# Modulation of layer 0's gate and of layer 1 moved from TensorE to row products summed on VectorE, and GpSimd's low parts of the first z pieces put ahead of the first inverse

## The reference, cut to what matters

```python
def ada_mod(cond, w, b):
    m = jax.nn.silu(cond) @ w + b
    return jnp.split(m[..., None, :], 3, axis=-1)

for i in range(DEPTH):
    shift, scale, gate = ada_mod(c, ada_w[i], ada_b[i])
    c_shift, c_scale, c_gate = ada_mod(c_ctx, ada_w[i], ada_b[i])
    h = rms_norm(x, norm_w[i]) * (1.0 + scale) + shift
    hc = rms_norm(ctx, norm_w[i]) * (1.0 + c_scale) + c_shift
    ...                       # i = 0: ab_mixer, i = 1: dn_mixer
    x = x + gate * o
    if need_ctx_out:
        ctx = ctx + c_gate * oc
```

## Time and profile before

| | |
|---|---|
| median of 3 runs | 2652.07 us (2651.2 to 2652.84) |
| the profiled execution | 2654.93 us, its span 2653.1 us |
| mean granted clock of TensorE | 0.96 of full speed |
| PE busy | 2447.0 us, 92% |
| DVE busy | 1028.2 us, 39% |
| ACT busy | 1132.7 us, 43% |
| POOL busy | 1179.7 us, 44% |
| chain that ended last | PE 71%, POOL 12%, DVE 6% |
| DMA | 352.15 MB, mean 133 GB/s |

### The profile page before, as it was taken

How to read it: one execution, slowest core, us unless ns; L and a number is a source line. 1 busy time by engine, 2 the same in 40 slices (tenths; PEclk the granted TensorE clock), 3 DMA queues, 4 the chain that set the end, 5 groups by cost and what they waited for, 6 DMA issues and landing times.

```text
span 2653.1 us, 59556 instructions
## 1 busy us (share of the span) xinstructions
PE 2447.0 (92%) x26092; PEld 2019.1 (76%) x26092; DVE 1028.2 (39%) x2211; ACT 1132.7 (43%) x2034; POOL 1179.7 (44%) x653
## 2 busy tenths in 40 slices
PE   6899999999999968999999999999999999986997
PEld 1477777777778847788878887888788878875997
DVE  1222222232230066444444444444444444443222
ACT  3423333333342245465346445643564356433443
POOL 2232333332335554643664365436544654451444
PEclk9899999999999969999999999999999999998999
DMA  9645444554443123223222322232223222314653
GB/s 397 259 168 195 170 182 183 207 199 189 167 183 95 56 87 106 89 66 105 96 97 66 105 96 95 68 105 91 97 71 105 89 96 74 105 49 172 226 182 121
DMA packets 98915, 352.15 MB, mean 133 GB/s; under 512 B 10720, under 2 KB 15200, under 8 KB 96224
## 3 DMA queue, kind: packets, MB, share of 16 engines
q1 hardware_dynamic: 98656, 348.34, 37.2%
HBM read 336.11 MB, written 12.19 MB: 131 GB/s over the span
## 4 chain that ended last, share of the span: by engine, by line
PE 71%; POOL 12%; DVE 6%; issue 4%; ACT 4%; DMA 3%; SPq 0%; POOLq 0%; DVEq 0%; ACTq 0%
PE bank L550 8%; PE bank L552 8%; PE bank L551 8%; PE bank L819 5%; PE bank L713 4%; PE bank L715 4%; PE bank L714 4%; POOL wl L401 4%; PE bank L526 3%; POOL scratch L2127 3%; PE bank L753 3%; POOL scratch L2147 3%; PE bank L754 3%; PE bank L755 3%; PE bank L1125 2%
## 5 line engine op out<-in xcount | busy, mean ns | idle before, releaser
L401 POOL TENSOR_TENSOR wl<-raw,wh 128x1024 fp32r<-128x1024 f32 x214 | 512.1, 2400 | 777.1 <-ACT wh L396 777.1
L713 PE MATMUL bank<-hh,wh 128*128 128x512 f32 (+1 forms) x1040 | 410.4, 395 | 22.4 <-POOL hl L2117 17.7
L396 ACT ACTIVATE wh<-raw 128x1024 fp32r<-128x1024 f32 x233 | 246.2, 1059 | 377.0 <-PE bank L755 229.9
L342 POOL TENSOR_TENSOR wl<-raw,wh 128x1024 fp32r<-128x1024 f32 x85 | 208.0, 2459 | 421.3 <-ACT wh L337 421.3
L550 PE MATMUL bank<-hh,wh 128*128 128x512 f32 x960 | 386.7, 403 | 5.9 <-POOL wl L342 3.6
L715 PE MATMUL bank<-hh,wl 128*128 128x512 f32 (+1 forms) x1040 | 385.5, 371 | 0.0
L714 PE MATMUL bank<-hl,wh 128*128 128x512 f32 (+1 forms) x1040 | 384.4, 370 | 0.0
L552 PE MATMUL bank<-hh,wl 128*128 128x512 f32 x960 | 376.8, 392 | 0.0
L551 PE MATMUL bank<-hl,wh 128*128 128x512 f32 x960 | 376.3, 392 | 0.0
L713 PEld LDWEIGHTS bank<-hh,wh 128*128 128x128 f32 x1040 | 199.7, 192 | 61.5 <-POOL hl L2117 15.2
L753 PE MATMUL bank<-wh,hh 128*128 128x256 f32 x512 | 166.3, 325 | 79.8 <-POOL wl L401 79.8
(11 more groups left out here) (273 smaller groups left out, 4487.1 us busy)
## 6 DMA issues: line engine op xcount, KB each, us to landing
raw<-w_in SPq DMA_DIRECT2D x259, 512.0 KB, 3.6
raw<-w_ada SPq DMA_DIRECT2D x123, 512.0 KB, 6.0
raw<-w_out SPq DMA_DIRECT2D x84, 512.0 KB, 3.7
scratch<-w_ada SPq DMA_DIRECT2D x69, 512.0 KB, 6.0
scratch<-keep_g SPq DMA_DIRECT2D x16, 1024.0 KB, 6.1
scratch<-w_in SPq DMA_DIRECT2D x23, 512.0 KB, 6.9
scratch<-xT SPq DMA_DIRECT2D x2, 4096.0 KB, 12.6
keep_y<-scratch SPq DMA_DIRECT2D x30, 256.0 KB, 2.4
```

What stands on the lines that cost most here:

```text
L342: eng.tensor_tensor(fl[h % SPLIT], ring[ring_slot("half", h)], fh[h % SPLIT].bitcast(F32), ALU.subtract)\
L396: eng.activation(buffers(s)[0], raw[:, s % RAW, :], ACT.Copy).then_inc(sem("rear_hi"), 1)
L401: eng.tensor_tensor(buffers(s)[1], raw[:, s % RAW, :], buffers(s)[0].bitcast(F32), ALU.subtract)\
L713: pe.matmul(ps, w[:, k * P:(k + 1) * P], hhv[:, kk, t0:t1], start=first and k == k0, stop=False)
```

## The change

Three things.

**The later modulation goes to VectorE.** The weights of the 64 tiles (gate of layer 0, tiles 32 to 47, shift, scale and gate of layer 1, tiles 48 to 95) are stored transposed, output columns on the partitions, contraction along the row: `w_late`, in 128 units of 128x1024, first half of the contraction (b = 0) for all tiles, then second half. The condition comes as two rows spread over all partitions (`crow`, half of the contraction at a time), ScalarE puts SiLU on it. VectorE multiplies a unit with a row and sums along it (`tensor_tensor_reduce`), two pieces of 512, for both conditions, or for the latent one alone in layer 1's gate; the sums run on in `mod`. All `ada`, `ada_rows`, `ada_sum` and `ada_add` of the mixing loop go. `GAPS` says how many units stand at which of four places of a group on VectorE: ahead of the q norm, behind it, behind the normed v, at the end. 83 units stand in the mixing loop, three each behind the merges of the output tiles.

**The ring is split.** Halves use 4 slots, units the other 2; SyncE's one queue still carries both, and the load of a unit waits until the unit two before it is done.

**GpSimd in layer 1** makes the low part of z piece 0 before the last two couplings and that of piece 1 before the first inverse.

The diff, cut to its core:

```diff
+LATE = list(range(2 * KT, 6 * KT))
+UNITS = [(tile, b) for b in range(2) for tile in LATE]
+NLATE = len(LATE)
+GAPS = [(4, 1, 3, 3)] * 5 + [(4, 1, 3, 1), (4, 1, 3, 3), (4, 1, 3, 0)]
+PERTILE = 3
...
+    order = []
     for a in range(len(EARLY)):
-        eighths(a, 0, 8)
-        for h in SOONER.get(a, ()):
-            half(h)
-    for h in range(3, 4 * KVH):
-        half(h)
-    for g in range(GROUPS):
-        h0, a = 4 * KVH + 10 * g, len(EARLY) + 2 * g
-        for t in range(5):
-            half(h0 + 2 * t)
-            half(h0 + 2 * t + 1)
-            if t < 4:
-                eighths(a + t // 2, 4 * (t % 2), 4 * (t % 2) + 4)
-    for h in range(4 * KVH + 10 * GROUPS, NHALF0):
-        half(h)
-    return place
-
-
-PLACE = front_places()
-AT = {n: what for what, n in PLACE.items()}
+        order += [("mod", 8 * a + e) for e in range(8)]
+        order += [("half", h) for h in SOONER.get(a, ())]
+    slots = {what: n % RING for n, what in enumerate(order)}
+    for h in range(3, NHALF0):
+        order.append(("half", h))
+        slots["half", h] = h % RAW
+    for u in range(len(UNITS)):
+        order.append(("unit", u))
+        slots["unit", u] = RAW + u % (RING - RAW)
...
-            n = PLACE[kind, i]
-            if n >= RING:
-                was, w = AT[n - RING]
-                eng.wait_ge(sem("ada_done") if was == "mod" else sem("front_lo"), w + 1)
-            eng.dma_start(ring[n % RING], src).then_inc(sem(f"ring_in{n % RING}"), 16)
+            if PREVIOUS[kind, i]:
+                was, w = PREVIOUS[kind, i]
+                eng.wait_ge(sem({"mod": "ada_done", "half": "front_lo", "unit": "late_done"}[was]), w + 1)
+            slot = SLOT[kind, i]
+            eng.dma_start(ring[slot], src).then_inc(sem(f"ring_in{slot}"), 16)
...
+                for j in range(10):
+                    half_loads(w_in0, 0, h + j, h + j + 1)
+                    if n == 6 and j == 6:
+                        sp.wait_ge(sem("late_done"), NLATE)
+                        sp.dma_start(crow, cond_row[0:1, :, HALF * P:].to_broadcast([P, 2, HALF * P]))\
+                          .then_inc(sem("crow_in"), 16)
+                    steps = {1: 1, 3: 1, 6: 4, 7: 1, 8: 2, 9: 2} if n == 6 else {1: 1, 3: 3, 6: 2, 7: 1, 8: 2, 9: 2}
+                    some = 0 if n == 0 and j < 6 else steps.get(j, 0)
+                    some = min(some, NMIXED - u)
+                    unit_loads(u, u + some)
+                    u += some
+            unit_loads(u, NMIXED)
             half_loads(w_out0, HOUT, HOUT, HOUT + 4)
+            unit_loads(NMIXED, NMIXED + 2)
...
-            half_loads(w_out0, HOUT, HOUT + 4, NHALF0)
+            u = NMIXED + 2
+            for t in range(2, KT):
+                half_loads(w_out0, HOUT, HOUT + 2 * t, HOUT + 2 * t + 2)
+                some = min(PERTILE, len(UNITS) - u)
+                unit_loads(u, u + some)
+                u += some
+            unit_loads(u, len(UNITS))
...
-                pe.wait_ge(sem("mod_added"), a)
                 if n == 0:
                     pe.wait_ge(sem("k_root"), KVH)
-                ada(a, 0, 4, pb[2])
-                if n:
+                else:
                     pe.wait_ge(sem("gb_read"), n)
                 front_tile(h + 2, pb[1][:, :])
-                ada(a, 4, 8, pb[2])
                 pe.wait_ge(sem("q_squared"), n + 1)
                 pe.matmul(pb[3][:, :], ones[:, :], a_sq, start=True, stop=True).then_inc(sem("q_summed"), 1)
 
                 pe.wait_ge(sem("q_copied"), n + 1)
-                front_half(h + 4, pb[0][:, :], True, False)
-                ada_sum(a, pb[2])
-                front_half(h + 5, pb[0][:, :], False, True)
+                front_tile(h + 4, pb[0][:, :])
...
+            def cond_silu(b):
+                act.wait_ge(sem("crow_in"), 16 * (b + 1))
+                act.activation(crow, crow, ACT.Silu).then_inc(sem("crow_ready"), 1)
...
-                ada_rows(a, pb[2])
+                if n == 6:
+                    cond_silu(1)
...
+            def late(u):
+
+                tile, b = UNITS[u]
+                ring_wait(dve, "unit", u)
+                dve.wait_ge(sem("crow_ready"), b + 1)
+                if b:
+                    dve.wait_ge(sem("late_done"), u - NLATE + 1)
+                unit = ring[ring_slot("unit", u)]
+                both = tile < 5 * KT
+                bias = sm[:, SO["ada_b"][0] + tile:SO["ada_b"][0] + tile + 1]
+                for j in range(2):
+                    js = slice(j * T, (j + 1) * T)
+                    if j:
+                        dve.wait_ge(sem("late_half"), u + 1)
+                    elif u:
+                        dve.wait_ge(sem("late_done"), u)
+                    for c in range(0 if both else 1, 2):
+                        acc = mod[:, tile, c:c + 1]
+                        done = dve.tensor_tensor_reduce(unit[:, js] if c else pb[2][:, :], unit[:, js], crow[:, c, js], 1.0,
+                                                        acc if b or j else bias, ALU.mult, ALU.add, acc)
+                    if j == 0:
+                        done.then_inc(sem("late_half"), 1)
+                done.then_inc(sem("late_done"), 1)
...
+                lates(GAPS[n][0])
                 dve.wait_ge(sem("q_copied"), n + 1)
                 head_norm(a_q, smc("q_w"), "q_root", n + 1, "q_normed")
-                ada_add(a, pb[2])
+                lates(GAPS[n][1])
...
+                lates(min(PERTILE, len(UNITS) - NMIXED - PERTILE * t))
+            dve.wait_ge(sem("late_done"), len(UNITS))
...
+                    rear_split_lo(pool, base + 8)
                     coupling(n, 2)
                     coupling(n, 3)
+                    rear_split_lo(pool, base + 9)
                     first_inverse(n)
-                    for s in range(base + 8, base + 14):
+                    for s in range(base + 10, base + 14):
```

More of the change, by code:

```diff
@@ L168, in build @@
         fl = [wl[:, s, :] for s in range(SPLIT)]
-        xres = cut(KT * T).rearrange("p (k t) -> p k t", t=T)
+        xroom = cut(KT * T)
+        xres = xroom.rearrange("p (k t) -> p k t", t=T)
+        silc, mrow = xroom[:, 0:KT * 32], [xroom[:, KT * 32 + n * T:KT * 32 + (n + 1) * T] for n in range(2)]
         n_sq = [cut(T), cut(T)]
@@ L184, in build @@
         cut(KT * T)
-        front_room()
+        crow = front_room()[1]
         mc = cut(NMIX)
@@ L427, in _, with unit_loads @@
             sp.dma_start(sgub, sgu_b[0:1, :].to_broadcast([P, GROUPS * P])).then_inc(sem("mix_in"), 16)
+            sp.dma_start(crow, cond_row[0:1, :, 0:HALF * P].to_broadcast([P, 2, HALF * P])).then_inc(sem("crow_in"), 16)
+            def unit_loads(first, last):
+                for u in range(first, last):
+                    tile, b = UNITS[u]
+                    ring_load(sp, "unit", u, w_late[tile - LATE[0], b, :, :])
             half_loads(w_in0, 0, RING, HMIX)
+            unit_loads(0, 2)
@@ L1650, in b_merge, with lates @@
                 dve.tensor_tensor(xv[:, GROUPS + n, :], pb[7][:, :], a_gb, ALU.mult).then_inc(sem("b_merged"), 1)
+            unit = iter(range(len(UNITS)))
+            def lates(n):
+                for _ in range(n):
+                    late(next(unit))
             for n in range(GROUPS):
-                a = NEARLY + 2 * n
                 if n:
                     b_merge(n - 1)
+                lates(GAPS[n][0])
                 dve.wait_ge(sem("q_copied"), n + 1)
                 head_norm(a_q, smc("q_w"), "q_root", n + 1, "q_normed")
-                ada_add(a, pb[2])
+                lates(GAPS[n][1])
                 dve.wait_ge(sem("q_normed"), n + 1)
```

78 lines of the change are left out of this document (34 added, 44 removed).

## The result

The changed kernel takes **2677.95 us** (median of 4 runs, 2672.21 to 2685.11); the kernel before, on the same chip, 2651.64 us (2649.08 to 2652.84). The ratio is 1.0101, interval 1.0086 to 1.0116: slower by about 26 us. The forecast was 2672. A second set of 4 runs of the changed kernel gave 2682.6 us and 1.0119 (1.0104 to 1.0135).

What follows compares the result with a forecast made beforehand. TensorE was taken to bound the kernel nearly everywhere, with VectorE bounding full mixing groups after the change. Mixing loop -9, output tiles +43 and layer 1 -14 sum to +20 on the 2652.07 median: 2672 us, range 2598 to 2735.

Steps and rivals of the forecast that it cites:

- TensorE's 8.98 us a group: Mixing loop: removing two modulation blocks frees TensorE of 8.98 us a group, 73.8 to 64.8 if nothing new is late.
- The price of a product: VectorE's 128x512 product with its accumulator read takes 0.775 us, range 0.70 to 0.85.
- rival 3: Everywhere products run: they go at half speed, 1.4 us each, giving about 2890 us; chance 8%.
- Held up by GpSimd: Each GpSimd low part meeting VectorE's units costs it 2.1 us; some 8 of 10 in a full group, 16.8 us.
- rival 1: Output tiles and full groups: GpSimd does not block the products, giving 2594 us; chance 20%.
- Mixing loop, -9: Layer 0's eight mixing groups: VectorE bounds full groups, so they sum to 581 us against 590, -9 rather than -72.
- rival 4: New 4 us stalls drop TensorE's clock, 1.5 to 2 us each over 20 stalls: +35, 2707 us; chance 10%.
- Output tiles, +43: Layer 0's output tiles: three units after each make full-unit tiles 15.0 us against 10.88, +43 us in all.
- Layer 1, -14: Layer 1's 15 heads: the z wait goes, a 4.7 us wait comes before scan step 2's residual; -0.9 us a head.
- Rival 2: Layer 1: the mask gets in before GpSimd's low part, so -60 instead of -14, 2626 us; chance 12%.
- Opening: The kernel's opening: moved ring slots and 1 MB more condition rows change the time by 0, at worst +3 us.

Runs made afterwards that it cites:

- Experiment 3: The changed kernel with the condition's row read from PSUM in the output tiles and the discarded product sent to SBUF: 2640.76 us, ratio 0.9956.
- experiment 1: The kernel before with only GpSimd's reordering in layer 1 (low parts of two z pieces ahead of the first inverse), no VectorE products: 2650.04 us, ratio 0.9989.
- Experiment 4: The changed kernel with VectorE's first transpose and mask of the next head behind scan step 2 in layer 1: 2630.88 us, ratio 0.9916.
- experiment 9: The changed kernel with PSUM row in tiles, transposes behind scan step 2, and mixing group 6's unit loads and units put later: 2578.31 us, ratio 0.9717.
- three and two units: On experiment 9, the other mixing groups put three units ahead of the head norm and two behind, instead of four and one: 2576.62 us, ratio 0.972.
- experiment 6: The kernel before with GpSimd's two low parts ahead of the first inverse and VectorE's transposes behind scan step 2, no products: 2597.21 us, ratio 0.9797.

## Why the prediction was right

The forecast was 2672 and the time 2678 (first set) and 2683 (second), both in its range, slower as said; one of its terms was wrong. By its own steps:

- **TensorE's 8.98 us a group**: a group with costless products takes 63.67 instead of 64.8, so TensorE was given back 10.1. Where the other 1.1 come from no run shows.
- **The price of a product**: 0.775 forecast. In the mixing loop the next one starts 0.67 to 0.80 behind an unblocked one, 0.72 in the mean; the accumulator read has a median of 0.084 (forecast 0.10). Right to 8%, and rival 3 (1.4 us) is out. The rule of the Trainium skill (Vector Engine (DVE) Microarchitecture Reference, "Points that are easy to get wrong"), which the page states for `S2S2D2_STT`, didn't hold for this operation: with both sources in SBUF a product has a median of 748 to 760 ns, with one in PSUM a mean of 746.
- **Held up by GpSimd**: 6 to 8 products in each of groups 0 to 4, longer by 10 to 16 us a group (forecast 8 and 16.8), and 35 to 37 in the tiles, 50 us. Experiment 3 takes the cause away: rival 1 is what would be if it did not exist, and the tiles then take 162.3 against 159.1, as the forecast said (+3). The Trainium skill (SBUF — State Buffer, "Who interferes with whom") and the trace agree, for this operation too, and the hold-up goes by GpSimd's instruction, not by the product's length: 8 columns took 2.41 us beside a low part of 2.4.
- **Mixing loop, -9**: -15.4 in the first profile, -6.1 in the second, -5.7 to -6.7 in the four others with this loop. Group by group, forecast 67, 72, 72, 72, 67, 65, 90; measured 66.0, 70.2, 70.7, 70.2, 64.4, 63.7, 91.5, and in the second set 66.1, 70.2, 70.7, 70.4, 69.7, 63.7, 93.5. TensorE waits where it was forecast, at the q rotation (4.2 us in groups 1 and 2, 9.3 in group 6) and at the softmax (2.1 and 3.9 in groups 0 and 3). The waits are shorter than forecast, and slower matmuls that were not in the sum make up for it (see rival 4).
- **Output tiles, +43**: +40.5 and +39.5, at 14.65 a tile instead of 15.0.
- **Layer 1, -14**: this is the term that was wrong: -3.2 in the first profile, -0.7 in the second, -3.9 in experiment 1. The step that failed is that the stretch at clock 0.50, "worth some 1.5 us", "only moves behind the wait". The wait is 4.34 (forecast 4.7), 0.96 a head shorter than the z wait in the mean (the 4.7 was not "as long as before", which was 5.32). But the stretch does not move as a whole: in the head shown 3.3 us of its 6.8 lay in the wait before, now 0.9, so TensorE works in 5.9 us of it in place of 3.5. That costs 0.94 us a head, and 14 x (0.96 - 0.94) is about nothing. A head came out 0.07 us shorter, not 0.9.
- **Rival 2** rested on the mask alone. Experiment 4 shows that the mask was still held up where 47 us were won: what mattered was not how long the transpose and mask take but that the residual stood behind them in VectorE's queue. A wait of 2.4 us behind the same mask is left. The forecast named this place and did not price taking it away.
- **Rival 4** (the clock) was given 10% and its mechanism did come: the mean granted clock fell from 1.00 to 0.95 in group 2 and to 0.88 in tiles 3 to 6. In groups 0 to 6 TensorE was busy for 15 us more than at 63.67 a group, in the tiles for 15.6 us more than before, near the +35 priced. It is part of the times above and not on top of them, since the waits came out shorter than forecast; how much of it moved the end no run shows.

So the sum was right partly by luck. Opening, mixing loop, tiles and the rest were forecast at 0, -9, +43 and -14; the first profile has -4.8, -15.4, +40.5 and -3.2, the second -5.6, -6.1, +39.5 and -0.7. Layer 1 gave 11 to 13 less than said; the opening (5 us that lie within its spread over all kernels), the tiles (3) and in the first profile the mixing loop (6) made up for it.

## What to carry to other kernels

Work moved from TensorE to VectorE with both inputs in SBUF cost its own time here and one hold-up for each reading GpSimd instruction that it met; one input in PSUM took the hold-up away, which was worth 1.4% of the kernel. A load queue in order makes every slow consumer a brake on whatever is queued behind it: look for who gives back the buffer that the queue's next entry waits for. And when a wait goes and the same time appears at the next place, look for an instruction that only stands in line there: two edits worth nothing each gave 2% together.

The best version is the changed kernel with experiments 3, 4 and 9: 2578.31 us, 2.8% under the kernel before (with three and two units 2576.62, not told apart). The products' part in it, with the row in PSUM and the lighter group 6, is what it lies below experiment 6: 19 us, 0.7 to 0.8%.
